# The last expert block's rows are added on chip, and the gate modulation moves to GpSimd ahead of the store

## What is computed

```python
def expert_block(args):
    xblk, e = args
    return (jax.nn.silu(xblk @ w1[e]) * (xblk @ w3[e])) @ w2[e]

yb = lax.map(expert_block, (xb, blk_e)).reshape(n_blocks * MOE_BLOCK, D)
f = jnp.zeros_like(h).at[stok].add(yb[dest] * sgate[:, None].astype(h.dtype))
xl = xl + mod_l[5] * f.reshape(xl.shape)
return rmsnorm(xl, final_norm_w)
```

## Time and profile before

| | us |
|---|---|
| median of 3 runs (lowest, highest) | 2294.71 (2293.37, 2295.1) |
| profiled execution: span from its first to its last instruction | 2293.7 |
| TensorE, VectorE, ScalarE, GpSimd busy | 2168.2, 1560.9, 995.0, 529.9 |

### The profile page before, as it was taken

How to read it: one execution, slowest core, us unless ns; L and a number is a source line. 1 busy time by engine, 2 the same in 40 slices (tenths; PEclk the granted TensorE clock), 3 DMA queues, 4 the chain that set the end, 5 groups by cost and what they waited for, 6 DMA issues and landing times.

```text
span 2293.7 us, 33388 instructions
## 1 busy us (share of the span) xinstructions
PE 2168.2 (95%) x10792; PEld 1802.2 (79%) x10792; DVE 1560.9 (68%) x1933; ACT 995.0 (43%) x1219; POOL 529.9 (23%) x674
## 2 busy tenths in 40 slices
PE   5889999999999999999999999999799999999990
PEld 2679888888888888788888888788688888888870
DVE  2478555676557656767666766733788988988975
ACT  3234323233233323422222222332278888888862
POOL 0046434453544455111111111100000011011002
PEclk8999999999999999999999999999899999999995
DMA  9975552222222222777777776843599999999966
GB/s 385 389 206 153 171 162 85 85 82 75 85 85 76 81 83 65 223 241 231 221 221 248 219 224 201 268 141 130 202 388 404 420 416 416 419 417 420 418 286 238
DMA packets 327561, 532.31 MB, mean 232 GB/s; under 512 B 12465, under 2 KB 253617, under 8 KB 297553
## 3 DMA queue, kind: packets, MB, share of 16 engines
q1 hardware_dynamic: 293904, 393.91, 48.3%
q0 software_dynamic: 33600, 137.66, 16.9%
HBM read 494.79 MB, written 36.73 MB: 232 GB/s over the span
## 4 chain that ended last, share of the span: by engine, by line
PE 83%; DVE 3%; DMA 2%; POOL 1%; issue 1%; ACT 0%; ACTq 0%; DVEq 0%; POOLq 0%
PE ps L694 13%; PE ps L696 13%; PE ps L695 13%; PE ps L1040 8%; PE ps L1042 8%; PE ps L1041 8%; PE ps L918 3%; PE ps L919 3%; PE ps L920 3%; PE ps L798 2%; PE ps L977 2%; PE ps L979 2%; PE ps L978 2%; PE ps L1066 1%; DMA y<-block_outputs,dest_i 1%
## 5 line engine op out<-in xcount | busy, mean ns | idle before, releaser
L1579 DVE TENSOR_TENSOR w_lo<-raw,w_hi 128x1024 fp32r<-128x1024 f32 x272 | 352.0, 1294 | 354.8 <-ACT w_hi L1164 353.4
L1164 ACT CAST w_hi<-raw 128x1024 fp32r<-128x1024 f32 x272 | 285.0, 1048 | 582.5 <-PE ps L696 275.8
L694 PE MATMUL ps<-hl_hi,w_hi 128*128 128x512 f32 x1280 | 505.6, 395 | 1.4 <-DVE hl_lo L1645 1.4
L696 PE MATMUL ps<-hl_hi,w_lo 128*128 128x512 f32 x1280 | 498.5, 389 | 0.0
L695 PE MATMUL ps<-hl_lo,w_hi 128*128 128x512 f32 x1280 | 498.3, 389 | 0.0
L2030 DVE TENSOR_TENSOR e_lo<-e_raw,e_hi 128x1024 fp32r<-128x1024 f32 x384 | 453.3, 1218 | 51.6 <-ACT e_hi L1445 43.8
L1445 ACT CAST e_hi<-e_raw 128x1024 fp32r<-128x1024 f32 x384 | 397.2, 1058 | 81.6 <-PE ps L1042 81.5
L696 PEld LDWEIGHTS ps<-hl_hi,w_lo 128*128 128x128 f32 x1280 | 240.3, 188 | 50.6
L694 PEld LDWEIGHTS ps<-hl_hi,w_hi 128*128 128x128 f32 x1280 | 240.5, 188 | 49.1 <-issue 1.5
L695 PEld LDWEIGHTS ps<-hl_lo,w_hi 128*128 128x128 f32 x1280 | 240.6, 188 | 47.5
L1040 PE MATMUL ps<-e_hi,xe_hi 128*128 128x512 f32 x512 | 201.2, 393 | 0.1
(11 more groups left out here) (374 smaller groups left out, 3652.7 us busy)
## 6 DMA issues: line engine op xcount, KB each, us to landing
e_raw<-in_w_e SPq DMA_DIRECT2D x192, 1024.0 KB, 9.7
raw<-in_w_in SPq DMA_DIRECT2D x208, 512.0 KB, 3.8
ada<-in_w_ada POOLq DMA_DIRECT2D x64, 1024.0 KB, 6.8
ada_ring<-in_w_ada SPq DMA_DIRECT2D x32, 1024.0 KB, 14.1
raw<-in_w_out SPq DMA_DIRECT2D x32, 512.0 KB, 3.9
block_outputs<-y_sb POOLq DMA_DIRECT2D x32, 512.0 KB, 6.6
raw<-in_w_branch_hgrn SPq DMA_DIRECT2D x16, 512.0 KB, 3.9
raw<-in_w_branch_pool SPq DMA_DIRECT2D x16, 512.0 KB, 3.9
```

The costliest lines, as they stand in the source:

```text
L694: mm(dst, hi, rhs_hi[:, k, :], start=(k == 0), stop=False)
L696: last = mm(dst, lo, rhs_hi[:, k, :], start=False, stop=(k == KT - 1))
L1164: act_e.copy(w_hi[:, hslot, :], raw[:, slot, :]).then_inc(hi_done, 1)
L1579: tt(w_lo[:, hslot, :], raw[:, slot, :], w_hi[:, hslot, :].bitcast(F32), ALU.subtract).then_inc(split_done, 1)
```

## The change

- y_sb is multiplied with m5_row on GpSimd (two 128x1024 tensor_tensor, in place) before each half is stored. The loop runs over blocks 1 to 14 only, and block 15 is written out behind it. It has no turn_x(16), and y_copy(14) comes in the midst of its casts.
- Block 15's order is: up w1, down(14), up w3, 16 transposes of the identity, turn_act(15), then down(15) in two column halves, each over all four k. Its output is not stored: VectorE scales it with gate and m5_row out of PSUM into v_last, it is split into v_hi (ScalarE) and v_lo (VectorE), and TensorE adds it to the token tiles with one-hot matrices (slots_last, built from a saved column of token ids): 32 matmuls of 128x512 into PSUM, which VectorE adds to x2 (whole).
- y_d's block 15 is zero; the gathers of tiles 0 to 2 start when all stores have landed and the ring buffers that they overwrite are free, during down(15). Tile 3 reuses the buffers of tile 0, once join(0) has read them. The modulated rows are added straight to x2: tiles 0 and 1 on VectorE, tiles 2 and 3 on GpSimd.
- The sigmoid goes to act_u (act_sig is gone), the square root's table is loaded ahead of the tail, the result is built in x2 (o_sb is gone).

```diff
@@ TensorE
-            with pe.Fori(1, E) as e:
+            with pe.Fori(1, LAST) as e:
...
-            x_ready(E)
-            turn_act(E - 1)
-            pe.wait_ge(actT_rdy, E + 2)
-            pe.wait_ge(y_ev, 4 * E)
-            for q in range(8):
-                down_unit(E * 24 - 8 + q, (q + 4) % EH, q)
+            for u in range(16, 24):
+                up_unit(G_LAST + u, (G_LAST + u) % EH, u - 16, 1)
+            for _ in range(16):
+                pe.transpose(bank(UB, P), ident[:], ident[:])
+            turn_act(LAST)
+            pe.wait_ge(actT_rdy, LAST + 3)
+            pe.wait_ge(y_ev, 4 * E)
+            for u in range(24, 32):
+                half, k = (u - 24) // 4, u % 4
+                e_unit(G_LAST + u, (G_LAST + u) % EH,
+                       [(2 + 2 * half + n, n, actT_hi[:, k, :], actT_lo[:, k, :], k == 0, k == 3) for n in range(2)])
...
+            pe.wait_ge(slots_rdy, USED + 1)
+            for i in range(NTOK):
+                for half in range(2):
+                    if i == 1:
+                        pe.wait_ge(v_out, USED + 4)
+                    if i >= 2:
+                        pe.wait_ge(f_sum, 2 * (i - 2) + half + 1)
+                    for n in (2 * half, 2 * half + 1):
+                        dst = bank(((0, 1, 6, 7), (2, 3, 4, 5))[i % 2][n])
+                        cols = slice(n * 512, (n + 1) * 512)
+                        if i == 0:
+                            pe.wait_ge(v_hi_rdy, USED + n + 1)
+                        mm(dst, slots_last[:, i, :], v_hi[:, cols], start=True, stop=False)
+                        if i == 0:
+                            pe.wait_ge(v_split, USED + n + 1)
+                        last = mm(dst, slots_last[:, i, :], v_lo[:, cols], start=False, stop=True)
+                    last.then_inc(last_mm, 1)
@@ ScalarE
+            for u in range(AHEAD, 29):
+                last_hi(u)
+                if u == AHEAD + 3:
+                    act_hi(LAST - 1)
+                if u == AHEAD + 9:
+                    act_e.wait_ge(e_units, G_LAST + EH + 8)
+                    sig1(LAST)
+                if u == AHEAD + 17:
+                    y_copy(LAST - 1, LAST - 1, G_LAST + EH + 16)
+            act_hi(LAST)
+            for u in range(29, 32):
+                last_hi(u)
@@ VectorE
+            for u in range(AHEAD, 29):
+                last_lo(u)
+                if u == AHEAD + 3:
+                    act_lo(LAST - 1)
+                if u == AHEAD + 9:
+                    silu(LAST)
+            gate_up(LAST, G_LAST + EH + 24)
+            own.wait()
+            for i in range(NTOK):
+                own.did(ts(slots_last[:, i, :], iota[:], float(i * P), tok_last[:], ALU.add, ALU.is_equal))
+            act_lo(LAST)
+            own.wait()
+            dve.nop().then_inc(slots_rdy, 1)
+            for u in range(29, 32):
+                last_lo(u)
+            dve.wait_ge(rows_in, 7 * 16)
+
+            def join(i, buf):
+                step(tt(x2[:, i, :], x2[:, i, :], buf[:], ALU.add))
+
+            for n in range(4):
+                dve.wait_ge(e_units, G_LAST + EH + 28 + 4 * (n // 2))
+                cols = slice(n * 512, (n + 1) * 512)
+                stt(out=v_last[:, cols], in0=bank(2 + n), scalar=gate_tab[:, LAST:LAST + 1], in1=m5_row[:, cols],
+                    op0=ALU.mult, op1=ALU.mult).then_inc(v_out, 1)
             n_extra = dve.value_load(route_i[0:1, 7:8], min_val=0, max_val=NXTRA)
...
+            for n in range(4):
+                cols = slice(n * 512, (n + 1) * 512)
+                dve.wait_ge(v_hi_rdy, USED + n + 1)
+                tt(v_lo[:, cols], v_last[:, cols], v_hi[:, cols].bitcast(F32), ALU.subtract).then_inc(v_split, 1)
+
+            def whole(i):
+                for half in range(2):
+                    dve.wait_ge(last_mm, USED + 2 * i + half + 1)
+                    first = ((0, 6), (2, 4))[i % 2][half]
+                    cols = slice(half * D // 2, (half + 1) * D // 2)
+                    tt(x2[:, i, cols], x2[:, i, cols], ps[:, first:first + 2, :].rearrange("p b n -> p (b n)"), ALU.add
+                       ).then_inc(f_sum, 1)
...
+            dve.wait_ge(y_in[0], 32)
+            join(0, y_buf[0])
+            join(0, y_buf[1])
+            dve.nop().then_inc(t0_taken, 1)
+            dve.wait_ge(y_in[1], 16)
+            join(1, y_buf[2])
+            whole(0)
+            whole(1)
+            finish(0)
+            dve.wait_ge(t_sum, USED + 1)
+            whole(2)
+            finish(1)
+            dve.wait_ge(t_sum, USED + 2)
+            whole(3)
+            finish(2)
+            finish(3)
@@ GpSimd
-            def store(b):
+            def store(b, turn):
                 for n in range(2):
                     cols = slice(n * D // 2, (n + 1) * D // 2)
-                    pool.wait_ge(y_ev, b * 4 + (6 + 2 * n))
+                    pool.wait_ge(y_ev, turn * 4 + (6 + 2 * n))
+                    own.did(tt(y_sb[:, cols], y_sb[:, cols], m5_row[:, cols], ALU.mult))
+                    own.wait()
                     pool.dma_start(y_d[ds(b * BLK, BLK), cols], y_sb[:, cols]).then_inc(y_out, 16)
...
+            pool.wait_ge(y_out, 16 * (2 * LAST + NTOK))
...
+            pool.wait_ge(e_split, 2 * EP + G_LAST + 24)
+            gather_y(0, 0, y_buf[0]).then_inc(y_in[0], 16)
+            gather_y(1, 0, y_buf[1]).then_inc(y_in[0], 16)
+            pool.wait_ge(e_units, EH + G_LAST + 24)
+            gather_y(0, 1, y_buf[2]).then_inc(y0_in[0], 16)
+            gather_y(0, 2, y_buf[3]).then_inc(y0_in[1], 16)
+            for i in (1, 2):
+                pool.wait_ge(y0_in[i - 1], 16)
+                gather_y(1, i, y_buf[1 + i], ALU.add).then_inc(y_in[i], 16)
+            pool.wait_ge(t0_taken, USED + 1)
+            gather_y(0, 3, y_buf[0]).then_inc(y_in[3], 16)
+            gather_y(1, 3, y_buf[1]).then_inc(y_in[3], 16)
+            pool.wait_ge(y_in[2], 16)
+            tt(x2[:, 2, :], x2[:, 2, :], y_buf[3][:], ALU.add).then_inc(t_sum, 1)
+            pool.wait_ge(y_in[3], 32)
+            tail.did(tt(y_buf[0][:], y_buf[0][:], y_buf[1][:], ALU.add))
+            tail.wait()
+            tt(x2[:, 3, :], x2[:, 3, :], y_buf[0][:], ALU.add).then_inc(t_sum, 1)
```

More of the change, by code:

```diff
@@ L626, in _ @@
                 load_e(n, n % EP, piece(0, n))
-            with sp.Fori(1, E) as e:
+            with sp.Fori(1, LAST) as e:
                 for n in range(12):
                     load_e(e * 12 + (n - 4), (n + 2) % EP, piece(e, n) if n < 8 else piece(e - 1, n))
-            for n in range(8, 12):
-                load_e(E * 12 - 12 + n, n % EP, piece(E - 1, n))
+            for i in range(16):
+                load_e(L_LAST + i, (L_LAST + i) % EP,
+                       piece(LAST - 1, 4 + i) if 4 <= i < 8 else piece(LAST, i if i < 4 else i - 4))
             sp.wait_ge(table_rdy, 1)
@@ L1452, in sig1 @@
             def sig1(b):
-                act_e.wait_ge(u_rdy, b)
-                activate(act_sig[:], bank(0), ACT.Sigmoid).then_inc(sg_rdy, 1)
+                act_e.wait_ge(act_rdy, b)
+                activate(act_u[:], bank(0), ACT.Sigmoid).then_inc(sg_rdy, 1)
             def act_hi(b):
@@ L1461, in gate_of, with y_copy @@
                 return gate_tab[:, b:b + 1] if isinstance(b, int) else gate_tab[:, ds(b, 1)]
-            def y_copy(b, units):
+            def y_copy(b, turn, units):
                 act_e.wait_ge(e_units, units)
-                act_e.wait_ge(y_out, b * 32 + 16 * NTOK)
+                act_e.wait_ge(y_out, turn * 32 + 16 * NTOK)
                 for part in range(4):
@@ L1500, in _, with last_hi @@
                         x_hi(e + 1, q - 18)
-                y_copy(e - 1, e * 24 + (EH + 16))
-            act_hi(E - 1)
-            for q in range(AHEAD, 8):
-                e_hi_unit(E * 24 - 8 + q, q + 4, E * 32 + 16 * ((q // 2 + 2) // EP))
-            y_copy(E - 1, E * 24 + EH)
+                y_copy(e - 1, e - 1, e * 24 + (EH + 16))
+            def last_hi(u):
+                load, half = last_raw(u)
+                slot = load % EP
+                act_e.wait_ge(e_in[slot], 16 * (load // EP + 1) + E_BASE[slot])
+                act_e.wait_ge(e_units, G_LAST + u + 1)
+                act_e.copy(e_hi[:, (G_LAST + u) % EH, :], e_raw[slot][:, half, :]).then_inc(e_hi_done, 1)
+            for u in range(AHEAD, 29):
[10 more added lines that the diff above has]
+                last_hi(u)
             n_extra = act_e.value_load(route_i[0:1, 7:8], min_val=0, max_val=NXTRA)
@@ L2181, in _, with last_lo @@
                         x_lo(e + 1, q - 18)
-            act_lo(E - 1)
-            for q in range(AHEAD, 8):
-                e_lo_unit(E * 24 - 8 + q, q + 4)
+            def last_lo(u):
+                load, half = last_raw(u)
+                dve.wait_ge(e_hi_done, G_LAST + u + 1)
+                n = (G_LAST + u) % EH
+                tt(e_lo[:, n, :], e_raw[load % EP][:, half, :], e_hi[:, n, :].bitcast(F32), ALU.subtract
```

(10 more changed lines are left out.)

122 lines of the change are left out of this document (67 added, 55 removed).

## The result

The changed kernel takes 2319.13 us (median; 2317.89 to 2321.95) where the kernel before, run beside it, takes 2294.04 us (2293.36 to 2295.1). The ratio is 1.0109, with a 95% interval of 1.0097 to 1.0121: slower by 25 us. I had forecast 2298.0, in a range of 2284 to 2309.

What follows compares the result with a forecast made beforehand. TensorE, busy 95% of the span, was taken as the bound. The stage's loss of 11.7 us less the tail's gain of 8.4 gave +3.3 on 2294.7, so 2298.0 us, range 2284 to 2309.

Steps and rivals of the forecast that it cites:

- VectorE becomes the bound by 0.75 us a turn: Expert stage: two multiplies cost VectorE 4.3 us a turn against a slack of 3.6, so turns take 35.8 us.
- The wait that I had named: Expert stage: TensorE waits for e_lo, the weights' low part, once a turn near the seventh unit.
- The price of a multiply: GpSimd's 128x1024 multiply before each store: 2.34 us, with 2.54 kept for the range.
- The loss of 2.16 us for each: Expert stage: each GpSimd multiply makes a waiting VectorE subtraction lose 2.34 - 0.18 = 2.16 us.
- my criterion: Expert stage: VectorE's counted work, 31.5 us, plus the multiplies' hold, compared with the turn of 35.08 us.
- The stage's sum: Expert stage: 0.25 in the first turn, 9.0 in twelve more, 0.75 and 1.65 in block 15: +11.7 us.
- All else: Last block and tail: a gain of 8.4 us, from 1.9 plus 9.5 behind M less 3.0 from t to M.
- M: The last matmul, forecast at t+21.05, with the end of the span at M+46.4 against 55.9 us before.
- t: End of the last block's last up unit, forecast at 2217.85 + 11.7 us.
- A: Rival, expert stage: multiplies interleave with VectorE or cost it under 1.8 us each, TensorE loses nothing; 2286.3 us, chance 0.22.
- B: Rival, tail: full clock in down (-3), GpSimd's two sums not held by VectorE's final products (-4.6); 2290.4 us, chance 0.16.
- C: Rival, expert stage: a multiply takes 2.54 us (decided from 2.4), turns 36.2 to 36.3; 2306.5 us, chance 0.26.

Runs made afterwards that it cites:

- a_xlate: Changed kernel, both multiplies kept, third and fourth groups of the next block's token transposes moved 4 and 5 units behind the second: 2297.94 us, ratio 1.0011.
- a_dve_g: Changed kernel, VectorE scaling out of PSUM replacing ScalarE's copy and GpSimd's multiplies, next block's gather issued ahead of the store: 2286.01 us, ratio 0.9959.
- a_nomul: Changed kernel without GpSimd's two multiplies a block, so blocks 0 to 14 lack the modulation row: 2285.36 us, ratio 0.9958.
- a_dve: Changed kernel with VectorE applying gate and modulation row out of PSUM, replacing ScalarE's copy and GpSimd's multiplies: 2295.13 us, ratio 0.9999.
- a_best: a_dve_g plus own row buffers for tile 3's earlier gathers and one test around the extra-block loop on every engine: 2283.61 us, ratio 0.9954.

## Why the prediction was wrong, step by step

**Direction and place: partly.** That the multiplies hold VectorE, and that they cost more than the tail gives back, was right. The size was wrong by 21 us, and it was all in the stage.

**The step that failed** is "VectorE becomes the bound by 0.75 us a turn". I compared VectorE's work over a turn with the turn (slack 3.6 us). The slack that counts is that of one operation: x_lo(0), whose bank the third transposes need, 0.2 us. The rows for it were in the trace of before, and turn_x's wait for `xe_rdy` in the code; I read TensorE's waits, found none, and took this for slack. a_xlate and a_dve_g show that VectorE's capacity was never the limit. The wait that I had named, for e_lo near the seventh unit, does come, with 0.6 us in eleven of 13 turns, close to my 0.75. That is luck: it comes from subtractions that are late at this point while VectorE still idles 2.7 us a turn. Nor is it added to the loss: the turn grows by as much as x_lo is late, whether this wait is there or all but absent (1.9 us late and 1.9 longer in the mild turns, 2.3 and 2.2 in the others).

**The price of a multiply.** 2.34 us was near: the first takes 2.40 us undisturbed, against 4.62 for the sum of 2048 elements (forecast 4.46). The loss of 2.16 us for each was right for a multiply that falls amid the subtractions (the second adds 2.6 us to the first's 0.2 in most turns, 2.2 in the turn shown) and wrong for the first. I had let both meet VectorE at work, "once VectorE runs late"; but TensorE's stall gives VectorE its 2.7 us gap back each turn, and the first multiply falls into it. By my criterion with the measured hold (31.5 + 2.8 = 34.3 of 35.08) the change would have cost nothing in the stage. Two errors of opposite sign brought the forecast near the right direction; the criterion alone was worth 28 us.

**The stage's sum.** 11.7 us forecast. Measured against a_nomul: 28.4 + 0.7 up to the last y_copy, and 3.8 to the gate product, 32.9.

**All else** (last block, M, tail): right within 1 us of the total, by a_nomul's 2285.36 against the 2286.3 of the same sum without the multiplies. Inside it terms cancel. The loop over skipped blocks (forecast 4.0 us behind the last piece, 5.5 shown as issue) and the first gather of tile 3, whose issue was held by VectorE's join (2.99 us, not the 0.98 of rows 11), were too small: 2.8 us from M to the end. Down took about what was forecast: M at t + 22.0 (21.05). The issue of the xe gather behind the multiplies took 1.0 to 1.75 us and came some 5 us later in the turn than before, at no cost, as forecast.

**Rivals.** A's price was right and its condition false. B's first condition failed: behind idle stretches of TensorE of 4.5 and 1.4 us the granted clock was 0.50 (1.2 GHz) from 2252.4 to 2257.4 and then 1.00 (2.4 GHz) from 2257.8. Its second held in half: of GpSimd's last two sums one took 4.52 us and one 6.42. C named the right direction for the size but its mechanism, a dearer multiply, was not it: the first multiply takes 2.40 us, on C's threshold, and C's own turn (36.2 to 36.3) was passed by a full us. None of my cases had a due time inside the turn, so the range could not hold the result.

## What to carry to other kernels

When something delays an engine beside the bound one, don't compare its work with the length of a turn: take each of its results that the bound engine waits for, and read from the two timelines how long before its use it is ready. A bound engine without waits can have a slack of 0.2 us at one of them. Work for GpSimd with SBUF operands belongs where VectorE is idle or reads PSUM; and here the scaling that VectorE does on the way out of PSUM was cheaper than the one that GpSimd does in SBUF afterwards, once GpSimd's gather had been moved out of VectorE's subtractions.

## What the runs showed of the hardware

- The exclusion of VectorE and GpSimd can also delay an indirect DMA's issue: 7.42 us under unbroken two-SBUF-input subtractions in eleven of 13 turns of a_dve (7.07 to 7.42), 1.15 us in the two others, 1.14 us in the kernel before, 1.38 us among x_lo operations (which read PSUM). A 128x1 copy on GpSimd ranged from 0.18 us to 3.11. The issue of a plain DMA amid the same subtractions took 0.53 us.
- The same multiply, asked for within 0.2 us of the same moment of the turn, held VectorE's subtractions so that both multiplies together cost VectorE 2.4 us in two turns and 2.8 in eleven (turns of 36.9 and 37.3 us in the kernel after).
- VectorE's scaling of a 128x512 PSUM bank by a column and an SBUF row takes 2.72 us for four, against 2.42 us for ScalarE's four copies.
- A loop with seven skipped turns cost VectorE 5.4 us between two operations (6.9 us from v_last to v_lo in the kernel after, 1.5 in a_best).
